# Context tiles behind the queries, the low part on VectorE alone, and a reordered router chain

## The reference, cut to what matters

```python
h  = rms_norm(x,  g1) * (1 + sc1) + sh1          # 512 x 1024, from mod = silu(c) @ ada_w + ada_b
hc = rms_norm(xc, g1) * (1 + csc1) + csh1        # 256 x 1024
u  = h @ w_in                                    # 8 chunks of 256: a_v a_b a_c p_in q k v f_in
kc, vc = split(hc @ w_in[:, 5*256:7*256])        # the context only needs keys and values
y  = concat([short_conv(a_v, a_b, a_c), multiscale_pool(p_in),
             neighborhood_attention(q, k, v, kc, vc), fourier_mix(f_in)])
x  = x + g1m * (y @ w_out)
h2 = rms_norm(x, g2) * (1 + sc2) + sh2
scores = sigmoid(h2 @ router_w)                  # 16 experts in 4 groups: best group, then top 2
f  = sum over the 2 chosen experts of gate * ((silu(h2 @ w1[e]) * (h2 @ w3[e])) @ w2[e])
out = rms_norm(x + g2m * f, final_g)
```

## Time and profile before

| what | value |
|---|---|
| median of three runs | 598.28 us |
| profiled execution | 596.1 us, its span 594.3 us |
| TensorE matmul busy | 554.3 us (93%) |
| VectorE busy | 442.2 us (74%) |
| ScalarE busy | 323.2 us (54%) |
| GpSimd busy | 153.2 us (26%) |
| mean granted TensorE clock | 0.983 |

### The profile page before, as it was taken

One profiled execution on the slowest core, in us unless ns is written; L12 is line 12 of the kernel. 1 busy time (PEld: TensorE's weight loads), 2 busy tenths in 40 slices (PEclk: granted clock), 3 DMA queues, 4 the chain that ended last, 5 costly groups with the idle time before them and its releaser, 6 DMA issues.

```text
span 594.3 us, 7645 instructions
## 1 busy us (share of the span) xinstructions
PE 554.3 (93%) x2733; PEld 418.0 (70%) x2733; DVE 442.2 (74%) x576; ACT 323.2 (54%) x401; POOL 153.2 (26%) x138
## 2 busy tenths in 40 slices
PE   1789998999998999988998999999999999999995
PEld 1445873677676777856577888888888888778772
DVE  1358595345586545437979999999999999999868
ACT  4530134245434923145736876677866777866624
POOL 5000926133220700021343212333212333210060
PEclk9789999999999999989999999999999999999998
DMA  8999997369213720058779999999999999999565
GB/s 303 390 373 320 380 377 258 106 181 368 73 72 112 250 99 36 35 176 321 250 273 383 374 395 391 392 392 393 389 390 391 389 392 387 368 381 366 208 220 205
DMA packets 89178, 171.81 MB, mean 289 GB/s; under 512 B 5427, under 2 KB 18935, under 8 KB 89153
## 3 DMA queue, kind: packets, MB, share of 16 engines
q1 hardware_dynamic: 83010, 153.34, 72.0%
q10 hardware_dynamic: 2768, 9.97, 4.1%
q0 software_dynamic: 3376, 8.18, 3.8%
HBM read 158.06 MB, written 17.32 MB: 295 GB/s over the span
## 4 chain that ended last, share of the span: by engine, by line
PE 81%; DVE 6%; DMA 6%; ACT 3%; issue 2%; SPq 1%; DVEq 0%; ACTq 0%
PE psum L892 6%; PE psum L1224 4%; PE psum L1225 4%; PE psum L1226 4%; PE psum L1236 4%; PE psum L1235 4%; PE psum L1234 4%; PE psum L1251 4%; PE psum L1253 4%; PE psum L1252 4%; PE psum L900 3%; PE psum L937 3%; DMA w<-in_moe_w 3%; DMA ada<-in_ada_w 3%; PE psum L939 3%; PE psum L938 3%
## 5 line engine op out<-in xcount | busy, mean ns | idle before, releaser
L2144 DVE TENSOR_TENSOR w_lo<-w,w_hi 128x2048 fp32r<-128x2048 f32 x32 | 72.9, 2282 | 2.4 <-ACT w_hi L1636 2.4
L2133 DVE TENSOR_TENSOR w_lo<-w,w_hi 128x1024 fp32r<-128x1024 f32 (+2 forms) x30 | 68.8, 2294 | 0.0
L1627 ACT CAST w_hi<-w 128x2048 fp32r<-128x2048 f32 x30 | 57.3, 1914 | 15.1 <-PE psum L1236 10.8
L1636 ACT CAST w_hi<-w 128x2048 fp32r<-128x2048 f32 x32 | 60.3, 1922 | 5.3 <-PE psum L1253 3.0
L2127 DVE TENSOR_TENSOR w_lo<-w,w_hi_a 128x2048 fp32r<-128x2048 f32 (+1 forms) x30 | 51.5, 1756 | 3.1 <-ACT w_hi_a L1623 2.5
L765 POOL COPY idx<-idx 128x1 int32 (+1 forms) x14 | 13.7, 975 | 147.5 <-PE psum L1198 147.4
L1251 PE MATMUL psum<-w_hi,heT_hi 128*128 128x512 f32 x120 | 49.5, 412 | 0.8 <-DVE w_lo L2144 0.8
L1253 PE MATMUL psum<-w_hi,heT_lo 128*128 128x512 f32 x120 | 47.0, 392 | 0.0
L1225 PE MATMUL psum<-w_lo,xgT_hi 128*128 128x512 f32 x120 | 46.8, 390 | 0.0
L1252 PE MATMUL psum<-w_lo,heT_hi 128*128 128x512 f32 x120 | 46.7, 389 | 0.0
L1234 PE MATMUL psum<-w_hi,xgT_hi 128*128 128x512 f32 x120 | 46.7, 389 | 0.0
(11 more groups left out here) (351 smaller groups left out, 1260.5 us busy)
## 6 DMA issues: line engine op xcount, KB each, us to landing
w<-in_moe_w SPq DMA_DIRECT2D x32, 2048.0 KB, 14.4
w<-in_moe_w SPq DMA_DIRECT2D x32, 1024.0 KB, 14.1
ada<-in_ada_w SPq DMA_DIRECT2D x12, 2048.0 KB, 18.1
win<-in_w_in SPq DMA_DIRECT2D x8, 1024.0 KB, 14.4
expert_rows<-ysb ACTq DMA_DIRECT2D x15, 512.0 KB, 6.4
expert_rows<-zero SPq DMA_DIRECT2D x1, 5120.0 KB, 21.4
wout<-in_w_out SPq DMA_DIRECT2D x4, 1024.0 KB, 4.9
x<-in_x SPq DMA_DIRECT2D x2, 1024.0 KB, 9.6
```

The source lines that it names most:

```text
L1636: act.copy(w2_hi[:, :, hs], w2_sb[b][:, :, hs]).then_inc(w2_hi_ok[half], 1)
L2133: v.tensor_tensor(w3_lo[b][:, ks, :], w3_sb[b][:, ks, :], w3_hi[:, ks, :], ALU.subtract).then_inc(w3_lo_ok, n)
L2144: v.tensor_tensor(w2_lo[b][:, :, hs], w2_sb[b][:, :, hs], w2_hi[:, :, hs], ALU.subtract).then_inc(w2_lo_ok[half], 1)
```

## The change

It has two parts. The first reorders the twelve tiles: keys, values and queries of the tokens first (tiles 0 to 7), context keys and values last (8 to 11), with ScalarE's copies, its two extra steps and SyncE's waits renumbered to match. `load_win(2)` is issued ahead of `load_ada(6)`. Both halves of `hT_lo` are now made by VectorE, ahead of its first softmax step; GpSimd makes none. On TensorE the two modulation pieces 10 and 11 move behind the first and the second fill half. The second part is the router: the addition that ends `h2` moves from VectorE to GpSimd; the expert pick and one product move behind the rank matrices; TensorE waits for each `hot_0` by itself, and runs two filler matmuls instead of three.

```diff
@@ -330,7 +330,6 @@
         pj_dve = sem("pj_dve")
         h_hi_ok = sem("h_hi_ok")
         h_lo_dve = sem("h_lo_dve")
-        h_lo_gp = sem("h_lo_gp")
         w_hi_ok = sem("w_hi_ok")
         w_lo_ok = sem("w_lo_ok")
 
@@ -525,9 +524,9 @@
                 sp.dma_start(raw[:, h].rearrange("p a b -> p (a b)"),
                              bass.AP(tab_dram.tensor, h * TAB,
                                      [[RPB_R, 16], [1, ROWS], [1, RUN]])).then_inc(raw_in, 16)
-            load_ada(6)
             sp.wait_ge(turn_ok, 4)
             load_win(2)
+            load_ada(6)
             load_ada(7)
             load_ada(8)
             load_ada(9)
@@ -536,7 +535,7 @@
             load_ada(10)
             load_ada(11)
             for i in range(4, 8):
-                sp.wait_ge(*((kv_ok, (4, 10, 12)[i - 4]) if i < 7 else (pj_ok, 2)))
+                sp.wait_ge(*((kv_ok, (10, 12, 12)[i - 4]) if i < 7 else (pj_ok, 2)))
                 load_win(i)
 
             sp.wait_ge(kv_ok, 12)
@@ -710,10 +709,6 @@
             low_w(0)
             low_w(1)
 
-            gp.wait_ge(kv_ok, 12)
-            gp.wait_ge(h_hi_ok, 2)
-            gp.tensor_tensor(hT_lo[:, 4:KD, :], hT[:, 4:KD, :], hT_hi[:, 4:KD, :], ALU.subtract).then_inc(h_lo_gp, 1)
-
             gp.wait_ge(ada_dve, 8)
             gp.memset(zero[:], 0.0).then_inc(zero_ok, 1)
             gp.memset(z[:, :, 0:1], 0.0)
@@ -750,6 +745,8 @@
                 gp.tensor_tensor(h2[:, 1, cs_], x1[:, NT - 1, cs_], rows[:, SC2, cs_], ALU.mult).then_inc(scale_ok, 1)
             gp.wait_ge(logit_ok, NT + 1)
             link(gp.memset(xg[1][:], 0.0))
+            gp.wait_ge(scale_ok, 3)
+            gp.tensor_tensor(h2[:, 1, :], h2[:, 1, :], rows[:, SH2, :], ALU.add).then_inc(h2_ok, 1)
 
             gp.wait_ge(idx_ok, 1)
             for b in range(2):
@@ -905,18 +902,18 @@
             pe.wait_ge(win_in[0], 16)
             kv_tile(0, channel_tile(0, 0, hT, N, h_ok))
             kv_tile(1, channel_tile(0, 1, hT, N))
+            pe.wait_ge(win_in[1], 16)
+            for m_ in range(NT):
+
+                kv_tile(2 + m_, value_tile(1, lambda k: hT[:, k, m_ * P:(m_ + 1) * P]))
+            pe.wait_ge(win_in[2], 16)
+            kv_tile(6, channel_tile(2, 0, hT, N))
+            kv_tile(7, channel_tile(2, 1, hT, N))
             pe.wait_ge(hc_ok, 1)
-            kv_tile(2, channel_tile(0, 0, hcT, L))
-            kv_tile(3, channel_tile(0, 1, hcT, L))
-            pe.wait_ge(win_in[1], 16)
+            kv_tile(8, channel_tile(0, 0, hcT, L))
+            kv_tile(9, channel_tile(0, 1, hcT, L))
             for t in range(LT):
-                kv_tile(4 + t, value_tile(1, lambda k: hcT[:, k, t * P:(t + 1) * P]))
-            for m_ in range(NT):
-
-                kv_tile(6 + m_, value_tile(1, lambda k: hT[:, k, m_ * P:(m_ + 1) * P]))
-            pe.wait_ge(win_in[2], 16)
-            kv_tile(10, channel_tile(2, 0, hT, N))
-            kv_tile(11, channel_tile(2, 1, hT, N))
+                kv_tile(10 + t, value_tile(1, lambda k: hcT[:, k, t * P:(t + 1) * P]))
 
 
             def fill(n):
@@ -931,7 +928,7 @@
                     elif tile > N_ACT_FILL:
                         pe.wait_ge(pj_dve, tile - N_ACT_FILL)
                 if tile == 0:
-                    pe.wait_ge((h_lo_dve, h_lo_gp)[part], 1)
+                    pe.wait_ge(h_lo_dve, part + 1)
                 w_lo = win_lo[i % 4][:, :, half * P:(half + 1) * P]
                 for k in range(4 * part, 4 * part + 4):
                     pe.matmul(bank[7][:], win_hi[half][:, k, :], hT_hi[:, k, :], start=(k == 0), stop=False)
@@ -984,7 +981,7 @@
                                       pT[:, odd, i * P:(i + 1) * P], start=(i == 0), stop=(i == nb - 1))
                 m.then_inc(o_ok, 1)
 
-            pe.wait_ge(kv_free, 11)
+            pe.wait_ge(kv_free, 10)
             nf = 0
             for p in range(NP_ + 1):
                 if p < NP_:
@@ -993,17 +990,18 @@
                     pe.wait_ge(ada_dve, 8)
                 if p >= 1:
                     values(2 * p - 2)
-                else:
-                    modulation(10)
-                    pe.wait_ge(kv_free, 12)
-                    modulation(11)
                 fill(nf)
                 if p >= 1:
                     values(2 * p - 1)
+                else:
+                    modulation(10)
                 fill(nf + 1)
                 nf += 2
                 if p >= 1:
                     output(p - 1)
+                else:
+                    pe.wait_ge(kv_free, 12)
+                    modulation(11)
                 if more_fill(p):
                     fill(nf)
                     nf += 1
@@ -1146,7 +1144,7 @@
                 for _ in range(n):
                     pe.matmul(bank[5][:], ones[:], x1[:, 0, 0:512], start=True, stop=True)
 
-            keep_busy(3)
+            keep_busy(2)
             pe.wait_ge(prob_ok, 1)
             pe.wait_ge(sel_ok, 1)
             for t in range(NT):
@@ -1163,12 +1161,13 @@
                 if k >= 4:
                     pe.wait_ge(x0_ok, k - 3)
                 for t in range(NT):
+                    if k == 0:
+                        pe.wait_ge(hot0_ok, t + 1)
                     m = pe.matmul(bank[(0, 1, 4, 5)[k % 4]][:, 0:P], x1[:, t, k * P:(k + 1) * P], hot_0[:, t, :],
                                   start=(t == 0), stop=(t == NT - 1))
                 m.then_inc(x0_ps, 1)
 
             pe.wait_ge(rows_act, 8)
-            pe.wait_ge(hot0_ok, 1)
             for k in range(4):
                 first_rows(k)
             pe.wait_ge(hot_ok, 1)
@@ -1426,20 +1425,20 @@
                 b = bank[n % 6]
                 if n < 2:
                     m = act.copy(kT[:, n, :], b)
-                elif n < 4:
-                    m = act.copy(kcT[:, n - 2, :], b[:, 0:L])
                 elif n < 6:
-                    m = act.copy(vc_sb[:, n - 4, :], b[:, 0:GW])
+                    m = act.copy(v_sb[:, n - 2, :], b[:, 0:GW])
+                elif n < 8:
+                    m = act.activation(qT[:, n - 6, :], b, ACT.Copy, scale=SCALE)
                 elif n < 10:
-                    m = act.copy(v_sb[:, n - 6, :], b[:, 0:GW])
+                    m = act.copy(kcT[:, n - 8, :], b[:, 0:L])
                 else:
-                    m = act.activation(qT[:, n - 10, :], b, ACT.Copy, scale=SCALE)
+                    m = act.copy(vc_sb[:, n - 10, :], b[:, 0:GW])
                 m.then_inc(kv_free, 1)
-                if n == 10:
+                if n == 9:
                     act.wait_ge(ada_dve, 5)
                     high_w(0)
                     high_w(1)
-                if n == 7:
+                if n == 6:
 
                     act.wait_ge(h_ok, KD)
                     act.wait_ge(ada_dve, 4)
@@ -1812,6 +1811,12 @@
                         link(ins)
                 ins.then_inc(ada_dve, 1)
 
+            v.wait_ge(kv_ok, 8)
+            for i in range(2):
+                v.wait_ge(h_hi_ok, i + 1)
+                v.tensor_tensor(hT_lo[:, 4 * i:4 * i + 4, :], hT[:, 4 * i:4 * i + 4, :], hT_hi[:, 4 * i:4 * i + 4, :],
+                                ALU.subtract).then_inc(h_lo_dve, 1)
+
             def softmax_bias(u):
                 h, j = UNITS[u]
                 m0, m1, sg0 = KEYS[j]
@@ -1900,11 +1905,6 @@
                 if p < NP_:
                     softmax_bias(2 * p)
                     softmax_bias(2 * p + 1)
-                if p == 0:
-                    v.wait_ge(kv_ok, 12)
-                    v.wait_ge(h_hi_ok, 1)
-                    v.tensor_tensor(hT_lo[:, 0:4, :], hT[:, 0:4, :], hT_hi[:, 0:4, :], ALU.subtract
-                                    ).then_inc(h_lo_dve, 1)
                 if p == NP_ // 2 + 1:
                     head_pair(0)
                 if p < NP_:
@@ -2020,9 +2020,6 @@
             v.tensor_tensor(pairs[:, :, 3:5], b4[:, :, 0:2], b4[:, :, 2:4], ALU.add)
             link(v.tensor_tensor(pairs[:, :, 5:6], b4[:, :, 0:1], b4[:, :, 3:4], ALU.add))
             link(v.tensor_reduce(gs[:].rearrange("p t g -> p (t g)").unsqueeze(2), pairs[:], AX, ALU.max))
-            v.wait_ge(scale_ok, 3)
-            v.tensor_tensor(h2[:, 1, :], h2[:, 1, :], rows[:, SH2, :], ALU.add).then_inc(h2_ok, 1)
-
             def first_max(src, pri, shape, dst, tmp):
 
                 link(v.tensor_reduce(r1[:], src, AX, ALU.max))
@@ -2052,22 +2049,21 @@
                                      rc[:].rearrange("p t k e -> p (t k) e"), AX, ALU.add))
 
             ohf = oh[:].rearrange("p t k e -> p (t k) e")
-            v.tensor_scalar(hot_base[:, :, 0, :], ohf, tok[:, 0:1], None, ALU.mult)
-            v.tensor_tensor(hot_base[:, :, 1, :], ohf, tok_chunk[:].unsqueeze(2).to_broadcast([P, NT * 2, NE]), ALU.mult)
-            pick(expert[:], eno[:].unsqueeze(1).unsqueeze(1).to_broadcast(E2))
-            v.wait_ge(rank_ok, 1)
             v.wait_ge(sel_ok, 1)
             v.tensor_tensor(first_scale[:], sel[:, :, 0], st2[:, :, 4], ALU.mult)
```

(9 more changed lines are left out.)

## The result

The changed kernel takes 601.1 us (median of 20 runs, 599.18 to 604.47), against 598.42 for the kernel before (20 runs, 595.39 to 607.42). The ratio is 1.0047, 95% interval 1.0027 to 1.0066: slower by 0.5%, clear of the noise of these runs, though under the 1% that the prediction took as the least that can be told. The forecast was 600.4, and its two steps are both to be seen. The profiled execution has a span of 601.2 us against 594.3.

A forecast was written before the change was run, and what follows sets the result against it. Bound by TensorE's unbroken tiles to 97 us, then its wait for `hT_lo`, and in the router by VectorE's chain of small instructions. +1.7 - 0.1 + 0.5 = +2.1 us on 598.28 gives 600.4, range 595.6 to 603.8.

The forecast's parts named there:

- its two steps: First fill waiting for `hT_lo` (third fill half 1.7 us later); router comparison held until GpSimd's addition ends (0.9 us lost).
- Tiles and loads: Before the first fill: tiles unbroken to 97.2 us, no wait for query weights or for the second modulation's load.
- The term for piece 6: `ada` 6 loaded later makes VectorE's 24 multiply-adds end at 94.1 instead of 92.46 us.
- The low part: VectorE's multiply-adds and GpSimd's `win_lo` subtractions share a lock, first fill waits 2.55 us, third fill half starts 1.7 later.
- the chain behind the last modulation: Before the third fill half: VectorE's addition 0.64 us, GpSimd's five memsets 0.5, copy of `fT` 0.73, no longer under the fills.
- The router: `h2` addition on GpSimd holds VectorE's comparison, 0.9 us lost; 0.3 and 0.7 won behind it; sum -0.1.
- The clock: TensorE's two thinner stretches, behind the scores and before the rank matrices, may lower its clock: +0.5 us.
- Rival C: Clock falls behind one or both thin TensorE stretches, each for 6.8 us; about 605 us with both; 8%.
- A: Rival, both parts: small and late VectorE instructions slip past GpSimd, -0.9 and -2.2, 595.2 us; 12%.
- B: Rival, low part: VectorE gets the port between GpSimd's two subtractions and keeps it, no fill wait; 597.8 us; 18%.
- The sum of +2.1: Whole kernel: +1.7 for the low part, -0.1 for the router, +0.5 for the clock, in us.

The follow-up runs named there:

- tiles_ada6: The kernel before with the change's first part alone, but `load_ada(6)` put back ahead of `load_win(2)`; 597.8 us, ratio 1.0006 to the kernel before.
- after_warm5: The changed kernel plus four filler matmuls behind the first scores and five router filler pairs instead of two; 598.84 us, ratio 1.0028 to the kernel before.
- Router_only: The kernel before with the change's second part, the router, alone; 598.34 us, ratio 0.9998 to the kernel before.
- router_fused: The kernel before with the router part, but the last `h2` rows made by one VectorE multiply-add ahead of the sigmoid; 594.89 us, ratio 0.9970.
- router_one: The kernel before with the router part, GpSimd's `h2` addition replaced by a one-operand multiplication, output not the reference's; one run, 600.9 us.

## Why the prediction was right, and where it was off

**Tiles and loads.** Right: the tiles stayed unbroken, the query weights caused no wait, the second modulation none either. The term for piece 6 was right and is the root of the loss in the traces: with piece 6 first the wait for `hT_lo` is gone (tiles_ada6), with it late the wait stays though the tiles end as late (after_warm5).

**The low part, +1.7 in the sum.** The mechanism was as forecast, multiply-adds and both subtractions sharing one lock and the first fill waiting for them. In the execution after, the mark moved by 6.24 and not by 1.7, and 2.5 of that are the slower clock, priced apart below. The rest was too small in two places. I let the tiles end at 97.2 and `hT_lo` be ready 2.55 us behind the scores; there, no slower clock held the tiles up around 41 us, so they ended 1.8 us earlier, while the multiply-adds did not end earlier, and the wait was 4.05. And the chain behind the last modulation (forecast 1.87) cost 2.13. In after_warm5 the tiles ended at 97.8, near the 97.2 that I took, and the clock was at 1.00 from the scores to the mark. There the mark is 15.2, of which about 1 us is the fillers' own overrun, against 14.05 forecast. So the step is sized well for tiles that end as late as before and a clock that stays up; that the tiles end earlier when the clock is up around 41 us I left out.

**The router, -0.1.** Forecast: comparison held until GpSimd ends, `sel` 0.9 later, 0.3 and 0.7 won behind it. Measured: `sel` 0.89 later; the matmuls behind the index products start 12.97 us behind `biased` in after_warm5 against 13.14 before: -0.2. Behind `sel` alone that is 5.48 against 6.56, 1.1 won where 1.0 was forecast. Router_only at 0.9998 agrees, within its 0.3%.

**The clock, +0.5.** Mis-sized: in the profiled execution it fell behind both stretches, 2.5 us in the fill and 2.4 in the first products. I took from the one execution before that the router of before brings no fall ahead of the first products; four kernels that keep it show one (first products of 5.2 to 6.0 us), so at most the fall in the fill is the change's; router_fused, with the old tiles, had one of 1.6 us near there too. In the medians it is less: the fillers brought back 1.1 and 2.2 us of 2.8. Rival C was thus partly on, with each fall costing 2.4 or 2.5 and not 3.4.

**The rivals.** A (small instructions pass) is refuted by 2.32 us for 16 elements. B (VectorE keeps the lock once it has it) is refuted by tiles_ada6, where the two engines alternate, and by the two multiply-adds of 2.72 us in the change itself. The sum of +2.1 met a median 2.7 us higher (0.47% of 598.3 is 2.8): the low part and the router as priced, the clock mis-sized at +0.5 where the fillers put it at 1 to 2. The interval of the ratio, 1.6 to 3.9 us, holds both the forecast's 2.1 and the 2.7, so the time by itself does not tell these splits apart, and part of the closeness is luck.

## What to carry to other kernels

Before moving work between VectorE and GpSimd, look in the trace for a small two-operand VectorE instruction that ends with a GpSimd one: if there is one, an addition moved off VectorE's chain can cost its whole GpSimd time (2.3 us here) as soon as the chain's next instruction reads two SBUF tiles. A swapped load that nothing seems to wait for can push a long VectorE series under such an instruction; compare where the series ends with where GpSimd starts, to half a microsecond. And a new wait of TensorE, such as the 4.05 us here, is to be priced with and without the slower clock behind it; more than one execution of the kernel before has to be looked at, since a fall that one of them lacks may be in the others.

## What the runs showed of the hardware

- The two engines take turns when both have instructions waiting: VectorE, GpSimd, VectorE, GpSimd, each whole, 8.9 us for four that end 2.1 to 2.3 us apart (tiles_ada6). The Trainium skill, SBUF — State Buffer, section SBUF: two separate sides, gives the lock to whichever starts first, for the whole instruction; the turns agree with that, the next point does not.
- A GpSimd instruction with one SBUF operand did not hold a two-operand comparison to its end: 1.06 of 2.80 us (router_one, one execution).
- GpSimd's subtractions of 128x1024 took 2.4 us (2.39 in the middle of ten in the kernel before), a VectorE subtraction of twice the size 2.28. VectorE alone made both halves of the low part in 4.49 us (the change); before, they took 3.71 us of VectorE and 4.56 of GpSimd.
